# Where sublayers meet: the last half's copy behind the first low tile, and the embedding's last two copies behind the gate weights' high part

## The chip, the cores and the metric

The kernel runs on one core of one Trainium2 chip. The metric is the device time in microseconds (us); lower is better. A core has TensorE (PE, the matrix engine), VectorE (DVE), ScalarE (ACT), GpSimd (POOL) and a queue engine (SP) that issues the loads. Each takes its own instructions in the order of the program, and they meet through semaphores.

## The reference

One step of a decoder layer for 512 prompt tokens and 32 sample tokens (544 in all, in two halves of 272), model width 1024, one layer:

```python
def layer(x, p, lp, mix_fn):
    x = x + 0.5 * rmsnorm(swiglu(rmsnorm(x, lp['f1_pre']), lp['f1_in'], lp['f1_out']), lp['f1_post'])
    h = rmsnorm(x, lp['mix_pre'])
    gq, gk, gv, gg, la, sq, sk, sv = project(h, lp['w_in'], lp['gate_w'], lp['gate_b'])
    o_gla, o_sb, new_state = mix_fn(gq, gk, gv, la, sq, sk, sv)
    m = merge(o_gla, gg, o_sb, lp['gla_norm'], lp['sb_norm'], lp['w_out'], x.dtype)
    x = x + rmsnorm(m, lp['mix_post'])
    x = x + 0.5 * rmsnorm(swiglu(rmsnorm(x, lp['f2_pre']), lp['f2_in'], lp['f2_out']), lp['f2_post'])
    gate = jax.nn.sigmoid(rmsnorm(x, lp['ple_pre']) @ lp['ple_w_gate'])
    e = p.astype(x.dtype) @ lp['ple_w_up']
    x = x + rmsnorm(gate * e, lp['ple_post'])
    return x, new_state
```

Each sublayer's output is normed by its own sum of squares over the 1024 channels before it is added to x, and the new x is normed again before the next sublayer's products.

## The kernel before, in words

Channels lie on the 128 partitions, so x is 8 tiles of 128 channels by 544 tokens. Every product is done in three matmuls, of the high and low parts of both operands: activations as `a_hi` and `a_lo`, weights as a high and a low copy of what a load left in `raw`. ACT makes a high part (a rounded copy), DVE the low part (the difference). A result takes a ticket, which is one of two "quads" of four PSUM banks, in turn: ticket t has quad t % 2, and PE's `open_ticket` waits until the quad's last user has been copied out (`psum_free`).

The change lies where one sublayer ends and the next begins. There are three such edges: edge 0 (end of the first feed-forward block, then the mixer's input product), edge 1 (end of the output projection, then the second feed-forward block) and edge 2 (end of the second feed-forward block, then the gate product of the embedding). At an edge the work goes by halves of the tokens:

- PE does the last product by halves (`edge_last`). DVE copies or adds each finished half out of PSUM (`last_out(0)`, `last_out(1)`: `down_half` at edges 0 and 2, one instruction; `mix_half` at edge 1, two copies). ACT squares it (`edge_squares`), PE sums the squares over the partitions with a matmul against ones (`post_sum`), ACT turns the sum into `rstd` (`norm`).
- For each of the 8 tiles k of a half, DVE scales the output by `rstd` into `work` (L1619), adds it to x (L1625), and later makes `a_lo` of tile k - 1 (L1631). ACT makes `a_hi` (L1223) and squares x into `y` (L1225). DVE adds these squares for the next norm (L1641).
- PE's `edge_first` takes the next product's first two tickets together. For each half and each k it waits for `a_lo` of that tile and does 12 matmuls (2 tickets x 2 tiles x 3). Both quads must be free before its first matmul. It holds the second half's `post_sum` of the sublayer that ended, and behind k = 2 of its second half the first half's sum of the next norm (`pre_sum`, L573 and L574). Then `edge_second` does the third ticket.

At edge 2 four products of the embedding p @ w_up (`embed`, L695) stand on PE between `edge_last` and `edge_first`. ACT copies each of the four results out of PSUM into `e` (`e_tiles`, L1553), between its other work at the edge (`between`). The gate product's second weight block is split there too: high part on ACT (L1152), low part on DVE (L1599).

All orders are written out by hand; no scheduler moves them. The argument `between` is given at edge 2 alone, so that `if between` means edge 2 and `if not between` means edges 0 and 1.

Of the kernel before, what the change touches and what calls it, by code (L numbers as in the profile page):

```python
# [111 lines left out]
def build(nc, a, o):  # L112
# [13 lines left out]
    with ctx:  # L126
# [220 lines left out]
        def placed(name, st):  # L347

            w = W0[name] + st.c
            return PLACED.get(w, slot_pair(w)) if isinstance(st.i, int) else slot_pair(w)  # L350
# [17 lines left out]
        def ticket(st, name):  # L368


            base = T0[name]
            return base + st.n, st.parity(base), st.half(base)
# [136 lines left out]
        def _(pe):  # L509
            mm = nc.tensor.matmul  # L510

            def open_ticket(t, quad, use):

                pe.wait_ge(psum_free[quad], use)
# [4 lines left out]
            def weights(w):  # L519
                pe.wait_ge(sig["split_lo"], w + 1)  # L520
# [16 lines left out]
            def dense_half(quad, pair, tiles, k, n_k, rhs, half, width=P):  # L537

                stride, tok = tiles * width, slice(half * HALF, (half + 1) * HALF)
                for c in range(tiles):  # L540
                    cols = slice(k * stride + c * width, k * stride + (c + 1) * width)
                    for n, (wt, act) in enumerate(((pair[0], rhs[0]), (pair[0], rhs[1]), (pair[1], rhs[0]))):
                        last = mm(PS[0:width, 4 * quad + 2 * c + half, 0:HALF], wt[:, cols], act[:, k, tok],  # L543
                                  start=(k == 0 and n == 0), stop=(k == n_k - 1 and n == 2))
                return last
# [9 lines left out]
            def post_sum(j, half):  # L555


                quad, tok, summed = sum_quad[j], slice(half * HALF, (half + 1) * HALF), SUMMED[j]
                pe.wait_ge(sig["sq_used"], SQ_BASE[j] + summed)
                for k in range(summed - 1, KD):  # L560
                    if k == summed:
                        pe.wait_ge(sig["edge_sq"], 2 * (j // 2) + half + 1)
                    squares = sum_sq if k < summed else sq[:, k % 2, :]
                    last = mm(PS[:, 4 * quad + 2 + half, 0:HALF], ones[:], squares[:, tok],  # L564
                              start=(k < summed), stop=(k == KD - 1))
                last.then_inc(sig["sum_full"], 1)

            def pre_sum(j, half):


                quad, at_ = sum_quad[j], half * HALF
                pe.wait_ge(sig["pre_ready"], j - 2 + half + 1)
                mm(PS[:, 4 * quad + half, HALF:512], ones[:], sum_sq[:, at_:at_ + TAIL], start=True, stop=True)  # L573
                mm(PS[:, 4 * quad + 2 + half, HALF:2 * HALF - TAIL], ones[:], sum_sq[:, at_ + TAIL:at_ + HALF],  # L574
                   start=True, stop=True).then_inc(sig["sum_full"], 1)
# [20 lines left out]
            def edge_first(b, stage_no, sums=True):  # L596


                name = EDGES[b]
                both = [(ticket(Step(c), name), placed(name, Step(c))) for c in range(2)]  # L600
                weights(W0[name] + 1)
                for (t, quad, use), pair in both:
                    open_ticket(t, quad, use)
                for half in range(2):
                    for k in range(KD):
                        pe.wait_ge(sig["a_lo_ready"], A_BASE[stage_no] + 8 * half + k + 1)
                        for (t, quad, use), pair in both:
                            last = dense_half(quad, pair, 2, k, KD, (a_hi, a_lo), half)
                            if half and k == KD - 1:
                                last.then_inc(sig["psum_full"], 1)  # L610
                        if half and k == 2:
                            pre_sum(2 * b + 2, 0)
                        elif sums and not half and k == 0:
                            post_sum(2 * b + 1, 1)

            def edge_second(b, width=P):
# [527 lines left out]
        def _(act):  # L1144
# [17 lines left out]
            def split_edge(name, c, t):  # L1162

                st = Step(c)
                act.wait_ge(sig["psum_full"], t)
                split_into(placed(name, st), st, name, widths[W0[name] + c])
# [27 lines left out]
            def edge_squares(b, half):  # L1194


                j = 2 * b + 1
                name, c = LAST[b]
                t, quad, use = ticket(Step(c), name)
                tok = slice(half * HALF, (half + 1) * HALF)  # L1200
                if half == 0:
                    act.wait_ge(sig["sq_used"], SQ_BASE[j] + SUMMED[j])
                    act.wait_ge(sig["y_half"], b + 1)
                else:
                    act.wait_ge(psum_free[quad], use + 1)
                if SUMMED[j] == KD - 1:
                    ins = fn(sq[:, 1, tok], y[:, KD - 1, half, :], ACT.Square)
                else:
                    ins = fn(sq[:, :, tok], y[:, KD - 2:KD, half, :], ACT.Square)
                ins.then_inc(sig["edge_sq"], 1)  # L1210

            def edge(b, name, between=None):


                j, c0 = 2 * b + 1, VEC[name]
                edge_squares(b, 0)
                norm(j, 0)
                edge_squares(b, 1)
                for half in range(2):
                    for k in range(KD):  # L1220
                        act.wait_ge(sig["x_ready"], 16 * b + 8 * half + k + 1)
                        xt = x[:, k, half, :]
                        fn(a_hi[:, k, half * HALF:(half + 1) * HALF], xt, ACT.Copy,  # L1223
                           scale=vec[:, c0 + k:c0 + k + 1]).then_inc(sig["a_hi_ready"], 1)
                        fn(y[:, k, half, :], xt, ACT.Square).then_inc(sig["pre_sq"], 1)  # L1225
                        if half == 0 and k == (0 if between else 4):
                            norm(j, 1)
                        elif half == 1 and k == 4:
                            norm(j + 1, 0)
                        if between:  # L1230
                            between(half, k)
# [322 lines left out]
                   ACT.Copy).then_inc(psum_free[t % 2], 1)  # L1554

            def between(half, k):
                if half == 0 and k % 2:
                    e_tiles(k // 2)
                if half == 0 and k == 4:
                    split_edge("gate", 1, T0["f2_down1"] + KD)  # L1560
                if half and k == 2:
                    split_edge("gate", 2, T0["embed"] + 3)

# [3 lines left out]
            for n in range(3):  # L1567
# [3 lines left out]
                for c in range(2):  # L1571
                    k = 2 * n + c
# [3 lines left out]
                for c in range(2):  # L1576
                    k = 2 * n + c
# [13 lines left out]
        def _(dve):  # L1591
# [35 lines left out]
            def edge_low(b, half, k, pre, stage_no):  # L1627

                c, tok = VEC[pre] + k, slice(half * HALF, (half + 1) * HALF)
                dve.wait_ge(sig["a_hi_ready"], A_BASE[stage_no] + 8 * half + k + 1)  # L1630
                v.scalar_tensor_tensor(a_lo[:, k, tok], x[:, k, half, :], vec[:, c:c + 1], a_hi[:, k, tok].bitcast(F32),  # L1631
                                       ALU.mult, ALU.subtract).then_inc(sig["a_lo_ready"], 1)
# [12 lines left out]
            def edge(b, post, pre, stage_no, last_out, between=None):  # L1645


                last_out(0)
                for half in range(2):
                    dve.wait_ge(sig["rstd_ready"], 2 * (2 * b + 1) + half)  # L1650
                    for k in range(KD):
                        if k > 1:

                            dve.wait_ge(sig["x_ready"], 16 * b + 8 * half + k - 1)
                        edge_update(b, half, k, post)
                        if k > 2:
                            edge_add(b, half, k - 2)
                        elif half and k:

                            edge_add(b, 0, KD - 3 + k)  # L1660
                        edge_x(b, half, k)
                        if half == 0 and k == 0:
                            last_out(1)
                        if k:
                            edge_low(b, half, k - 1, pre, stage_no)
                        if between:
                            between(half, k)
                    edge_low(b, half, KD - 1, pre, stage_no)
# [498 lines left out]
            def between(half, k):  # L2167
                if half == 0 and k == 4:
                    split_edge("gate", 1)
                if half and k == 4:  # L2170
                    split_edge("gate", 2)
# [3 lines left out]
            for n in range(3):  # L2175
# [21 lines left out]
                for c in range(2):  # L2197
                    k = 2 * n + c
# [269 lines left out]
```

## Time and profile before

| what | value |
|---|---|
| median of 3 runs | 1255.69 us (1255.69 to 1261.52) |
| profiled execution, its own time | 1254.07 us |
| profiled execution, span of the core | 1252.3 us |
| PE busy | 1206.0 us, 96% of the span |
| PE weight loads busy | 1166.8 us, 93% |
| DVE busy | 601.6 us, 48% |
| ACT busy | 440.6 us, 35% |
| POOL busy | 104.5 us, 8% |
| PE idle on `e` before `edge_first` of edge 2 | 6.2 us |
| PE idle on `a_lo` at edges 0 and 1, together | 4.7 us |

The span is what the trace covers; the execution's own time is 1.8 us longer. Busy shares are means over the whole span, in which nearly all stretches are bound by PE. What the edges cost has to be read from PE's idle stretches there. The granted clock is that of TensorE, 1.00 being its full 2.4 GHz and 0.50 its lower level of 1.2 GHz.

### The profile page before, as it was taken

The page shows a single profiled execution, that of the slowest core. Times are in us where ns is not written, and L with a number is a line of the kernel's source. Part 1 is how long each engine was busy: PE and PEld are TensorE (multiplying, and loading weights), DVE is VectorE, ACT ScalarE, POOL GpSimd, SP SyncE. Part 2 cuts the span into 40 slices and gives each one's busy share as a digit, 9 for nine tenths or more (in the row PEclk, how much of TensorE's full clock was granted, in tenths as well). Part 3 has the DMA queues.
Part 4 walks back from the last instruction along what each step waited for, and adds up shares of the span by engine and source line. Part 5 has one row for each costly group of instructions (what it writes and reads, how often), then busy time and mean ns, then how long its engine had stood idle before and what let it go on. Part 6 is the DMA issues. An engine that isn't in the chain of part 4 may idle for free.

```text
span 1252.3 us, 22655 instructions
## 1 busy us (share of the span) xinstructions
PE 1206.0 (96%) x9582; PEld 1166.8 (93%) x9582; DVE 601.6 (48%) x810; ACT 440.6 (35%) x566; POOL 104.5 (8%) x147
## 2 busy tenths in 40 slices
PE   7999999999999899999998999999999999999895
PEld 6899999999999889999877698999999999999794
DVE  5443422234334857555378747544321344434737
ACT  4322222212223432312299745322221222223634
POOL 7100000000001002121040020000000000011002
PEclk9999999999999999999999999999999999999898
DMA  5223132332223122123055151223223222125102
GB/s 208 80 88 100 51 102 84 101 101 67 76 75 121 51 69 78 65 64 106 1 188 192 62 169 35 68 68 100 75 76 105 82 100 90 53 85 172 40 1 71
DMA packets 40804, 110.17 MB, mean 88 GB/s; under 512 B 4962, under 2 KB 7026, under 8 KB 40610
## 3 DMA queue, kind: packets, MB, share of 16 engines
q1 hardware_dynamic: 38930, 103.13, 25.0%
q0 software_dynamic: 1232, 5.01, 1.2%
q8 instruction: 49, 0.80, 0.3%
q10 hardware_dynamic: 576, 1.08, 0.2%
q14 instruction: 17, 0.14, 0.0%
HBM read 103.57 MB, written 5.64 MB: 87 GB/s over the span
## 4 chain that ended last, share of the span: by engine, by line
PE 88%; ACT 5%; DVE 4%; issue 1%; DMA 1%; SPq 0%; DVEq 0%; ACTq 0%
PE PS L532 70%; PE PS L543 10%; PE PS L788 1%; DVE w_lo L1599 1%; PE PS L564 1%; PE PS L815 1%; ACT w_hi L1152 1%; DMA raw<-in_w_in 1%; PE PS L695 0%; PE PS L845 0%; PE PS L889 0%; PE PS L964 0%; PE PS L848 0%; DVE extra L2230 0%; ACT proj L1359 0%
## 5 line engine op out<-in xcount | busy, mean ns | idle before, releaser
L532 PE MATMUL PS<-a_hi,w_hi 128*128 128x272 f32 x1680 | 352.1, 291 | 12.0 <-DVE w_lo L1772 7.2
L532 PE MATMUL PS<-a_lo,w_hi 128*128 128x272 f32 x1680 | 349.5, 289 | 0.0
L532 PE MATMUL PS<-a_hi,w_lo 128*128 128x272 f32 x1680 | 347.9, 288 | 0.0
L532 PEld LDWEIGHTS PS<-a_hi,w_hi 128*128 128x128 f32 x1680 | 264.6, 189 | 16.9 <-issue 11.9
L1599 DVE TENSOR_TENSOR w_lo<-raw,w_hi 128x2048 fp32r<-128x2048 f32 (+3 forms) x94 | 180.9, 1924 | 188.8 <-ACT w_hi L1152 188.8
L532 PEld LDWEIGHTS PS<-a_hi,w_lo 128*128 128x128 f32 x1680 | 265.8, 190 | 0.0
L532 PEld LDWEIGHTS PS<-a_lo,w_hi 128*128 128x128 f32 x1680 | 265.6, 190 | 0.0
L1152 ACT ACTIVATE w_hi<-raw 128x2048 fp32r<-128x2048 f32 (+3 forms) x95 | 151.5, 1595 | 75.0 <-PE PS L532 63.7
L1255 ACT ACTIVATE work<-work 128x544 f32<-128x544 f32 x44 | 29.0, 659 | 325.2 <-DVE work L1697 325.2
L1697 DVE TENSOR_TENSOR work<-PS,rstd 128x544 f32<-128x544 f32 x43 | 31.2, 726 | 210.2 <-PE PS L532 201.3
L532 PE MATMUL PS<-h_hi,w_hi 128*128 128x272 f32 x584 | 121.1, 289 | 0.0
L532 PE MATMUL PS<-h_lo,w_hi 128*128 128x272 f32 x584 | 120.8, 288 | 0.0
L532 PE MATMUL PS<-h_hi,w_lo 128*128 128x272 f32 x584 | 119.5, 286 | 0.0
L532 PEld LDWEIGHTS PS<-h_lo,w_hi 128*128 128x128 f32 x584 | 91.9, 189 | 0.0
L532 PEld LDWEIGHTS PS<-h_hi,w_lo 128*128 128x128 f32 x584 | 91.7, 188 | 0.0
L532 PEld LDWEIGHTS PS<-h_hi,w_hi 128*128 128x128 f32 x584 | 91.1, 188 | 0.0
L543 PE MATMUL PS<-a_hi,w_hi 128*128 128x272 f32 x224 | 66.8, 298 | 11.0 <-ACT e L1553 6.2
L2277 POOL COPY sum_sq<-sq 128x544 f32<-128x544 f32 x4 | 3.2, 792 | 763.1 <-ACT sq L1273 685.7
L543 PE MATMUL PS<-a_hi,w_lo 128*128 128x272 f32 x224 | 65.8, 294 | 0.0
L543 PE MATMUL PS<-a_lo,w_hi 128*128 128x272 f32 x224 | 65.5, 292 | 0.0
L543 PEld LDWEIGHTS PS<-a_hi,w_hi 128*128 128x128 f32 x224 | 43.1, 192 | 11.9 <-issue 11.8
L1705 DVE TENSOR_TENSOR h_lo<-work,h_hi 128x544 f32 (+1 forms) x43 | 31.2, 726 | 38.9 <-ACT h_hi L1257 38.9
(419 smaller groups left out, 1562.1 us busy)
## 6 DMA issues: line engine op xcount, KB each, us to landing
raw<-in_f_in SPq DMA_DIRECT2D x86, 512.0 KB, 4.5
raw<-in_f_out SPq DMA_DIRECT2D x32, 384.0 KB, 3.4
raw<-in_f_out SPq DMA_DIRECT2D x32, 320.0 KB, 3.1
raw<-in_w_rest SPq DMA_DIRECT2D x40, 256.0 KB, 2.9
raw<-in_w_out SPq DMA_DIRECT2D x8, 512.0 KB, 4.2
raw<-in_ple_w_gate SPq DMA_DIRECT2D x8, 512.0 KB, 4.1
x<-in_x SPq DMA_DIRECT2D x8, 272.0 KB, 6.9
out<-x SPq DMA_DIRECT2D x8, 272.0 KB, 2.2
```

Source lines behind the costliest of these rows:

```text
L532: last = mm(PS[0:width, 4 * quad + 2 * c + half, 0:HALF], wt[:, cols], act[:, k, half * HALF:(half + 1) * HALF], start=(k == 0 and n == 0) ...
L543: last = mm(PS[0:width, 4 * quad + 2 * c + half, 0:HALF], wt[:, cols], act[:, k, tok], start=(k == 0 and n == 0), stop=(k == n_k - 1 and n ...
L564: last = mm(PS[:, 4 * quad + 2 + half, 0:HALF], ones[:], squares[:, tok], start=(k < summed), stop=(k == KD - 1))
L788: last = mm(PS[:, 2 + hh, tok], k_[r, tok], q_[r, tok], start=True, stop=True)
L815: last = mm(PS[:, 7, n * 256:n * 256 + 256], kl_batch[:, 2 * part + n, :], gv_new[:, p * 256:(p + 1) * 256], start=True, stop=True)
L1152: fn(pair[0][:, 0:width], raw[:, slot, 0:width], ACT.Copy).then_inc(sig["split_hi"], 1)
L1255: fn(gs, gs, ACT.Silu).then_inc(sig["silu_ready"], 1)
L1599: v.tensor_tensor(pair[1][:, 0:width], raw[:, slot, 0:width], pair[0][:, 0:width].bitcast(F32), ALU.subtract).then_inc(sig["split_lo"], 1)
L1697: v.tensor_tensor(gs, banks(quad, 0, 2), r, ALU.mult).then_inc(sig["g_ready"], 1)
L1705: v.tensor_tensor(h_lo[:, hs, :].rearrange("p a t -> p (a t)"), flat(us), h_hi[:, hs, :].bitcast(F32).rearrange("p a t -> p (a t)"), ALU.s ...
L2277: g.tensor_copy(sum_sq[:], sq[:, 0, :] if j else flat(y[:, 0])).then_inc(sig["sq_used"], 1)
```

## The change

Four places are edited; nothing is added to or taken from the computation.

1. On PE, at edges 0 and 1, the second half's `post_sum` moves from behind tile k = 0 to behind tile k = 1.
2. On ACT, at edges 0 and 1, the squares of the last half (`edge_squares(b, 1)`) move from ahead of the first tile to behind tile 1. Edge 2 keeps its order.
3. On DVE, at edges 0 and 1, the last half's copy (`last_out(1)`) moves from behind x of tile 0 to behind the first low tile.
4. On ACT, at edge 2, `e_tiles(2)` and `e_tiles(3)` move from tiles k = 5 and k = 7 to directly behind the high part of the gate product's second weight block, at k = 4.

```diff
@@ PE, edge_first @@
                         if half and k == 2:
                             pre_sum(2 * b + 2, 0)
-                        elif sums and not half and k == 0:
+                        elif sums and not half and k == 1:
                             post_sum(2 * b + 1, 1)
@@ ACT, edge @@
                 norm(j, 0)
-                edge_squares(b, 1)
+                if between:
+                    edge_squares(b, 1)
                 for half in range(2):
...
                         fn(y[:, k, half, :], xt, ACT.Square).then_inc(sig["pre_sq"], 1)
+                        if not between and half == 0 and k == 1:
+                            edge_squares(b, 1)
                         if half == 0 and k == (0 if between else 4):
                             norm(j, 1)
@@ ACT, between @@
-                if half == 0 and k % 2:
+                if half == 0 and k in (1, 3):
                     e_tiles(k // 2)
                 if half == 0 and k == 4:
                     split_edge("gate", 1, T0["f2_down1"] + KD)
+                    e_tiles(2)
+                    e_tiles(3)
@@ DVE, edge @@
                         edge_x(b, half, k)
-                        if half == 0 and k == 0:
+                        if between and half == 0 and k == 0:
                             last_out(1)
                         if k:
                             edge_low(b, half, k - 1, pre, stage_no)
+                        if not between and half == 0 and k == 1:
+                            last_out(1)
```

ACT at edge 2, from `e_tiles(1)` on, before the change. `h_lo<-raw` is the high part of the gate weights (it is kept in memory of `h_lo`), `e<-PS` is an `e_tiles`:

```order
L1553 ACTIVATE e<-PS 128x1088
L1223 ACTIVATE a_hi<-x,vec 128x272
L1225 ACTIVATE y<-x 128x272
L1152 ACTIVATE h_lo<-raw 128x2048
L1223 ACTIVATE a_hi<-x,vec 128x272
L1225 ACTIVATE y<-x 128x272
L1553 ACTIVATE e<-PS 128x1088
L1223 ACTIVATE a_hi<-x,vec 128x272
L1225 ACTIVATE y<-x 128x272
L1223 ACTIVATE a_hi<-x,vec 128x272
L1225 ACTIVATE y<-x 128x272
L1553 ACTIVATE e<-PS 128x1088
```

The same place in the changed kernel:

```order
L1556 ACTIVATE e<-PS 128x1088
L1224 ACTIVATE a_hi<-x,vec 128x272
L1226 ACTIVATE y<-x 128x272
L1152 ACTIVATE h_lo<-raw 128x2048
L1556 ACTIVATE e<-PS 128x1088 x2
L1224 ACTIVATE a_hi<-x,vec 128x272
L1226 ACTIVATE y<-x 128x272
L1224 ACTIVATE a_hi<-x,vec 128x272
L1226 ACTIVATE y<-x 128x272
L1224 ACTIVATE a_hi<-x,vec 128x272
L1226 ACTIVATE y<-x 128x272
```

The two last copies now stand ahead of the high parts of tiles 5, 6 and 7; they stood behind those of tiles 5 and 7.

DVE at edge 1, from x of tile 0 on, before the change. `y<-PS` is the copy of the last half, and the line with `a_lo` is the first low tile:

```order
L1625 TENSOR_TENSOR x<-work,x 128x272
L1746 COPY y<-PS 128x272 x2
L1619 SCALAR_TENSOR_TENSOR work<-y,vec,rstd 128x272
L1625 TENSOR_TENSOR x<-work,x 128x272
L1631 SCALAR_TENSOR_TENSOR a_lo<-x,vec,a_hi 128x272
```

The same place in the changed kernel:

```order
L1630 TENSOR_TENSOR x<-work,x 128x272
L1624 SCALAR_TENSOR_TENSOR work<-y,vec,rstd 128x272
L1630 TENSOR_TENSOR x<-work,x 128x272
L1636 SCALAR_TENSOR_TENSOR a_lo<-x,vec,a_hi 128x272
L1753 COPY y<-PS 128x272 x2
```

The scaling, the sum and the low part now stand ahead of the copies. Edge 0 has the same order with one `y<-PS,y` (L1734) in place of the two copies. On ACT the squares `sq<-y` move at both edges from ahead of `a_hi` of tile 0 to behind the square of tile 1.

## Rows read from the trace of the kernel before

**Rows 1.** The page, part 4: shares of the chain that ended last, by engine
```profile
PE 88%; ACT 5%; DVE 4%; issue 1%; DMA 1%; SPq 0%; DVEq 0%; ACTq 0%
```

**Rows 2.** PE's waits: line, releaser, us in total, times, longest
```profile
PE PS L543 <- ACT e L1553: 6.2, 1, 6.2
PE PS L543 <- DVE a_lo L1631: 4.7, 2, 2.6
...
PE PS L564 <- ACT sq L1207: 1.4, 1, 1.4
```

**Rows 3.** Chain at edge 1: start us, us, what
```profile
759.25 0.80 DVE y L1746 x2
...
760.08 0.66 ACT sq L1209
...
761.83 1.75 PE PS L543 x12
763.58 1.38 PE PS L564 x6
764.95 15.10 PE PS L543 x120
```

**Rows 4.** DVE in order of time, edge 1: start, us, line, operation
```profile
757.03 0.44 DVE L1625 TENSOR_TENSOR x<-work,x 128x272 f32<-128x272 f32 x1
...
760.49 0.44 DVE L1625 TENSOR_TENSOR x<-work,x 128x272 f32<-128x272 f32 x1
...
762.49 0.50 DVE L1631 SCALAR_TENSOR_TENSOR a_lo<-x,vec,a_hi 128x272 fp32r<-128x272 f32 x1
```

**Rows 5.** ACT in order of time, edge 1: the norm of the second half
```profile
766.42 0.47 ACT L1178 ACTIVATE rstd<-PS,eps 128x272 f32<-128x272 f32 x1
```

**Rows 6.** DVE in order of time, edge 0
```profile
416.59 0.44 DVE L1734 TENSOR_TENSOR y<-PS,y 128x272 f32<-128x272 f32 x1
416.94 0.50 DVE L1619 SCALAR_TENSOR_TENSOR work<-y,vec,rstd 128x272 f32<-128x272 f32 x1
417.47 0.44 DVE L1625 TENSOR_TENSOR x<-work,x 128x272 f32<-128x272 f32 x1
417.94 0.50 DVE L1631 SCALAR_TENSOR_TENSOR a_lo<-x,vec,a_hi 128x272 fp32r<-128x272 f32 x1
```

**Rows 7.** PE in order of time, edge 0: first matmul, its idle time ahead
```profile
418.59 0.41 PE L543 MATMUL PS<-a_hi,w_hi 128*128 128x272 f32 x1 [2.04 <-DVE a_lo L1631]
```

**Rows 8.** Chain at edge 2
```profile
1181.97 18.98 PE PS L543 x132
1200.95 0.41 PE PS L573 x2
```

**Rows 9.** ACT in order of time, edge 2
```profile
1171.47 1.91 ACT L1152 ACTIVATE h_lo<-raw 128x2048 fp32r<-128x2048 f32 x1
...
1180.66 1.06 ACT L1553 ACTIVATE e<-PS 128x1088 f32<-128x1088 f32 x1
```

**Rows 10.** DVE in order of time, edge 2: weights' low part, low tiles, x
```profile
1173.41 2.29 DVE L1599 TENSOR_TENSOR h_lo<-raw,h_lo 128x2048 fp32r<-128x2048 f32 x1 [3.04 <-ACT h_lo L1152]
...
1176.38 0.44 DVE L1625 TENSOR_TENSOR x<-work,x 128x272 f32<-128x272 f32 x1
1176.73 0.50 DVE L1631 SCALAR_TENSOR_TENSOR a_lo<-x,vec,a_hi 128x272 fp32r<-128x272 f32 x1
...
1191.36 0.50 DVE L1631 SCALAR_TENSOR_TENSOR a_lo<-x,vec,a_hi 128x272 fp32r<-128x272 f32 x1
```

**Rows 11.** Windows: stretch, length, busy PE, PEld, DVE, ACT, POOL, PEclk, DMA
```profile
418.59:421.49 2.90, 2.90 (x13) 2.90 (x14) 2.87 (x8) 1.81 (x6) 0.00 (x0) 0.53 0.00 0
759.22:763.58 4.36, 1.75 (x13) 1.78 (x14) 4.01 (x10) 2.97 (x7) 0.00 (x0) 1.00 0.00 0
1175.75:1181.97 6.22, 0.00 (x2) 0.03 (x1) 6.01 (x16) 4.42 (x9) 0.00 (x0) 0.84 0.50 169
1181.97:1186.80 4.83, 4.83 (x21) 4.83 (x22) 4.83 (x14) 3.87 (x7) 0.00 (x0) 0.50 0.02 3
```

## The prediction

> **What bounds the kernel now.** I read the page first. The chain that ended last lies on PE for 88% of the span [rows 1], so nearly every stretch is paid in matmuls, and a reordering can give back only time in which PE stands still or runs at its lower clock. The second view is what PE waits for [rows 2]. Two of its entries lie at the edges that the change touches: 6.2 us at edge 2, where the first gate product waits for a copy of the embedding (`e`), and 4.7 us at edges 0 and 1 together, where `edge_first` waits for its first low tile. The larger of those two is 2.6 us, so the other is 2.1. The third view is the timeline of each engine around the three edges, and the fourth is the granted clock there [rows 11]. What is to be seen in them stands with each edge below.
>
> **Edge 2: the two embedding copies (ACT).** PE's last embedding matmul ends at 1175.75 and the first gate matmul starts at 1181.97: the idle window has that length, 6.22 us, with no PE work in it [rows 11]. What ends it is the last of the four copies: it starts at 1180.66 and takes 1.06, so it ends at 1181.72 [rows 9], and PE follows 0.25 later [rows 8]. That copy is late only because ACT reaches it behind tile 7, and tile 7 waits for DVE. DVE in turn had been held until 1175.70 by the low part of the gate weights (1173.41 + 2.29) [rows 10]. In the changed order both copies stand behind the weights' high part, which ends at 1171.47 + 1.91 = 1173.38 [rows 9]. The first copy can run there at once, to about 1174.4. The second needs the last embedding product, which ends at 1175.75. It starts at about 1175.78, ends 1.06 later at 1176.84, and PE follows by the same 0.25, at 1177.09. The weights' low part is then ready by 1.4 us. The start comes 1181.97 - 1177.09 = 4.88 us earlier, and the idle time falls from 6.22 to 1.34.
>
> Does PE find its tiles? The low tiles of k = 0 to 3 were done before DVE took the weights' low part, and that of k = 4 ends at 1176.73 + 0.50 = 1177.23 [rows 10]. From there on DVE makes a low tile in about 1.5 us (16 instructions in 6.01 us, four to a tile [rows 11]), and PE uses one in 15.10 / 120 x 12 = 1.51 us [rows 3]. PE starts four tiles behind DVE, so it doesn't catch up. DVE's later halt for the second weight block is the place to look at: the low tile k = 4 of the second half ends at 1191.36 + 0.50 = 1191.86 [rows 10]. PE at full clock needs it after 12 tiles and the first `pre_sum`, at about 1177.09 + 0.24 + 12 x 1.51 + 0.55 = 1196.0. There are 4 us to spare. What ACT has waiting behind the two copies is the high part of tile 5, which needs x of tile 5; that is done at 1176.38 + 0.44 = 1176.82 [rows 10], and ACT is free at 1176.84. So holding ACT for the last embedding product costs nothing. The last three tiles of the second half wait for the norm behind `pre_sum`, so they move along with it.
>
> The clock is the second part of this edge. Behind the idle 6.22 us PE ran its first 4.83 us at a granted clock of 0.50, and did 21 matmuls in them, 0.23 each against 0.126 at 1.00 [rows 3, 11]. Its 132 matmuls up to `pre_sum` took 18.98 [rows 8]. At edge 1 the same kind of matmuls, 12 and then 120, took 1.75 + 15.10 = 16.85 at full clock, and there the engine had stood still 2.61 us just before them, without losing its clock [rows 3, 11]. An idle 1.34 us, in the midst of dense matmuls on both sides, is half of that, so I take full clock: 18.98 - 16.85 = 2.13 us more. Edge 2 gives 4.88 + 2.13 = 7.01 us. The bounds of the clock term are 0 (it still falls, and PE pays as much as before) and 2.13.
>
> The Trainium skill, page "TensorE: Matmul & The Clock Gate", section "A second HAM failure mode: psum-queue depth-cycling", speaks against taking that whole term: a PE that idles briefly between groups of matmuls can fall back to the lower clock again and again. By that rule the sum would lack 2.13 us; by the row of edge 1, which kept 1.00 through a longer pause, it has it. The row decides for me, and the rule is a rival below.
>
> **Edge 1: squares, copy and sum.** Before, x of tile 0 was done at 757.03 + 0.44 = 757.47 [rows 4], but ACT had the last half's squares ahead of `a_hi`, and these had to wait for DVE's copies, which start at 759.25 right behind PE's last matmul (at 761.83 - 2.61 = 759.22) and end at 759.25 + 0.80 = 760.05. The squares ended at 760.08 + 0.66 = 760.74 [rows 2, 3], `a_hi` and `a_lo` of tile 0 followed, and PE started at 761.83 [rows 3]. In the new order `a_lo` of tile 0 is ready by about 758.8, before PE ends the last product. This doesn't let PE start at 759.23, though. `edge_first` opens both quads before its first matmul, and one of them is the quad of the last output product, which DVE's copies free at 760.05. DVE reaches them in time: x, scaling, x and low part are done some 1.8 us after 757.03. With 0.14 us for the signal (the low tile of edge 0 ends at 418.44, PE starts at 418.59 [rows 6, 7]) PE starts at 760.2. The gain is 761.83 - 760.2 = 1.63 us, out of the 2.61 of idle time. The bounds are 1.5 (a signal as slow as the 0.25 of edge 2 [rows 8, 9]) and 1.65.
>
> Behind that, the second low tile must follow. After the copies DVE does scaling and x of tile 2 (before, the x in this position started at 760.49 [rows 4]), then the low part at 760.49 + 0.35 = 760.84, done at 761.34. PE wants it after 12 matmuls in 1.75, at 761.95, so it is 0.6 us early. It started at 762.49 before [rows 4]: all of DVE's work from there on is 1.65 us earlier, as is PE's. The moved `post_sum` costs its 1.38 us behind tile 1 in place of tile 0 [rows 3]; no matmul is added. It ends at 760.2 + 1.75 + 1.51 + 1.38 = 764.84. ACT asks for it before its norm at 766.42 [rows 5] less 1.65, which is 764.77: 0.1 us of waiting, in front of a norm that DVE needs only 3 us later. Edge 1 gives 1.6 us.
>
> **Edge 0.** Here DVE isn't held by PE: PE's last product of this edge ends at about 416.55, and the copy ran at 416.59 [rows 6], right behind x of tile 0. In the new order scaling starts at 416.59, x 0.53 later (as 416.94 to 417.47), the low part 0.35 behind that (as 416.59 to 416.94), at 417.47, and the copy behind it, between 0.35 and 0.50 later by the spacings and lengths of these rows; I take 0.41, so 417.88. It ends at 418.32 and frees the quad. PE starts 0.14 later, at 418.46, where it started at 418.59 [rows 7]. So the copy takes the place of the low tile as what PE waits for, and the gain is 0.13 us. The clock there is 0.53 in the first 2.90 us [rows 11]; `post_sum` moves from the end of that stretch to behind it and tile 1 moves in, which exchanges matmuls of one engine in a stretch that isn't made longer. I take nothing for it. The bounds are 0 and 1.4 us, the latter if the clock doesn't fall: 13 matmuls in 2.90 against 1.75 for 12 at edge 1, and the slow rest of the sum. ACT waits for the later `post_sum` there, by about 1 us, ahead of the norm; DVE is still at tile 5 then and uses that norm about 3 us later.
>
> **The sum.** 7.01 + 1.6 + 0.13 = 8.75 us. Everything behind each edge is PE's own work, or the same chain behind `pre_sum`, and moves along. No load moves past another one: the gate weights' loads are released by the low parts, which stay where they are. The profiled execution took 1254.07, so 1254.07 - 8.75 = 1245.3 for an execution like it. The median of the runs shown is 1.6 us above it, so 1246.9 for a median. I take 1246.9.
>
> **The rivals.**
> (a) *The short pause at edge 2 still costs the clock* (10%). For it: edge 0, where a pause of 1.4 us for the squares came shortly ahead of the one of 2.04, got 0.53 [rows 2, 7, 11]. Against it: edge 1. Then edge 2 gives 4.88 alone, the sum is 6.6 and the time 1249.1.
> (b) *The edges 0 and 1 give nothing, or edge 2 is held elsewhere* (13%). The first part alone costs 1.7: 1248.6. For the second, the place is PE's start behind the weights' low part or a tile: if the tiles of the second half are late, each microsecond of it is given back one to one, up to the whole 7. The time would be about 1252. Against it: the 4 us of slack at tile 4 of the second half.
> (c) *Slower* (2%). The one mechanism that I can name is ACT held by the wait of the second copy at edge 2, with `a_hi` of tiles 5 to 7 queued behind it. The price is one to one for what the last embedding product ends later than x of tile 5, less PE's lead of four tiles. By the rows the product ends 1.07 us before x of tile 5 (1175.75 against 1176.82) and the copy fits in exactly. The wait decides from about 6 us on, when tile 5 would be late on PE. To lose 0.5% it would have to be some 20 us.
> (d) *The forecast, with the clock at full level* (75%).
>
> **How the numbers follow.** A measurement of this kernel can tell about 0.5% (6.3 us, so 1249.4) from no change. Case (d) lies clearly below it, (a) and the milder half of (b) just below, where the scatter of a median may put them on either side. Faster 0.86, same 0.12, slower 0.02. The range takes (d) with the clock kept at edge 0 (1246.9 less 1.4, and less the 1.6 that a median may not have over the profiled execution: 1243.9) and, on the other side, (a) with edge 1 at nothing (1250.8). That is 1243.8 to 1250.8.
>
> **What would show it.** In the trace of the changed kernel PE's wait for `e` at edge 2 should be 1.3 us in place of 6.2, the granted clock 1.00 behind it, and 132 matmuls should take about 16.9. At edge 1 PE's pause should be about 1.0 us, ended by the copy `y` and no longer by `a_lo`. At edge 0 it should still be 1.9, ended by `y` as well, with a low clock behind it. The prediction is wrong if the clock at edge 2 is 0.50 again, if a wait for `a_lo` appears in `edge_first`, or if PE stands still behind `post_sum`.

## The result, and the profile after

The changed kernel took 1247.64 us (median of 5, 1247.5 to 1248.74); the kernel before took 1259.18 (median of 5, 1255.69 to 1261.52). The ratio is 0.9935, with a 95% interval of 0.9919 to 0.995. A repetition of both on one chip gave 0.9936 (0.9922 to 0.995). That is 8.2 us less of 1256. The two medians of five are 11.5 us apart, but the five executions of the kernel before are spread over 5.8 us, and larger sets of it (17, 7 and 11 executions) have medians of 1255.43, 1255.56 and 1256.2; so I go by the ratio. The prediction had 8.75 less, and 1246.9 us.

The profiled execution of the changed kernel has a span of 1245.2 us, 7.1 us less than before. Its waits of PE, as in [rows 2] (line, releaser, us in total, times, longest):

```profile
PE PS L543 <- DVE y L1741: 2.0, 1, 2.0
...
PE PS L543 <- ACT e L1556: 1.4, 1, 1.4
PE PS L564 <- ACT sq L1207: 1.2, 1, 1.2
PE PS L543 <- DVE y L1753: 1.1, 1, 1.1
```

The wait for `e` at edge 2 fell from 6.2 to 1.4 us. At edges 0 and 1 PE waits no longer for `a_lo` but for DVE's copy `y`: 1.1 us at edge 1 (2.6 before), and 2.0 at edge 0, as before [rows 7]. The chain at edge 2, which answers to [rows 8]:

```profile
1164.14 10.56 PE PS L695 x84
...
1174.72 1.09 ACT e L1556
...
1176.05 16.84 PE PS L543 x132
1192.89 0.41 PE PS L573 x2
```

The last copy starts when the last embedding product ends and PE follows it. The windows of the pause and of the 132 matmuls, in the columns of [rows 11]:

```profile
1174.70:1176.05 1.35, 0.00 (x0) 0.03 (x1) 1.35 (x4) 1.33 (x2) 0.00 (x0) 1.00 0.25 39
1176.05:1192.89 16.84, 16.84 (x133) 16.84 (x134) 15.59 (x36) 8.07 (x17) 0.00 (x0) 1.00 0.18 60
```

The granted clock is 1.00 in both, where it was 0.50 behind the pause before [rows 11]. The chain at edge 1, which answers to [rows 3]:

```profile
755.83 3.76 PE PS L543 x30
...
759.62 0.80 DVE y L1753 x2
...
760.66 3.27 PE PS L543 x24
763.93 1.37 PE PS L564 x6
765.30 9.82 PE PS L543 x78
```

ACT's squares and the low tile are gone from the chain; only DVE's copy stands between PE's last product and its next one.

To compare executions, I cut each trace at the same points of the program. "Edge 0" and "edge 1" run from the first half's sum of squares (L564) to the first matmul of tile 2; "edge 2" from the first embedding matmul to `pre_sum` (L573); "head" is what lies ahead of edge 0, "tail" what lies behind edge 2's `pre_sum`. Each is the difference of two starts in the chain. For edge 2 before: 1200.95 - 1162.79 = 38.16. In the order of before, tile 2 has no row of its own: the chain's row starts with tile 1, and I add the 1.51 us of its 12 matmuls. For edge 0 before: 422.81 + 1.51 - 413.95 = 10.37. All in us; "slow" marks a spell of TensorE's clock at 0.50 within an edge.

| profile | head | edge 0 | edge 1 | edge 2 | tail | span |
|---|---|---|---|---|---|---|
| before | 413.95 | 10.37 slow | 12.36 | 38.16 slow | 51.4 | 1252.3 |
| before, second | 415.28 | 10.20 slow | 12.37 | 38.47 slow | 51.3 | 1254.0 |
| changed | 415.91 | 8.81 | 10.84 | 31.17 | 52.3 | 1245.2 |
| changed, second | 414.63 | 8.82 | 10.84 | 31.17 | 52.3 | 1243.8 |
| changed, third | 413.89 | 10.33 slow | 10.83 | 31.18 | 52.2 | 1244.5 |

Edge 1 gives 1.53 us, to a few hundredths the same each time. Edge 2 of the changed kernel repeats to 0.01 us, that of the kernel before differs by 0.3 (its slow 132 matmuls took 18.98 and 19.29), so edge 2 gives 7.0 to 7.3. Edge 0 moves by 1.5 us among executions of the changed kernel, and the head by 1.3 and 2.0 among executions of one and the same kernel. The tail is the same within each kernel and 0.9 us longer in the changed one.

### The profile page after: what moved, and what is told of

The parts are those of the page before. It is cut to its first block, busy times and chain, and to the rows that moved or that the text cites. A ratio compares the mean times of both kernels' runs of the same rounds, so it can differ in the third digit from the quotient of the medians.

```text
span 1245.2 us, 22655 instructions
## 1 busy us (share of the span) xinstructions
PE 1204.4 (97%) x9582; PEld 1164.5 (94%) x9582; DVE 601.9 (48%) x810; ACT 441.2 (35%) x566; POOL 104.5 (8%) x147
## 4 chain that ended last, share of the span: by engine, by line
PE 89%; DVE 5%; ACT 4%; DMA 1%; issue 1%; ACTq 0%; SPq 0%; DVEq 0%
PE PS L532 70%; PE PS L543 10%; PE PS L788 1%; PE PS L695 1%; PE PS L964 1%; DVE w_lo L1604 1%; PE PS L564 1%; PE PS L815 1%; ACT w_hi L1152 1%; DMA raw<-in_w_in 1%; DMA raw<-in_f_in 1%; PE PS L845 0%; PE PS L889 0%; PE PS L848 0%; DVE extra L2237 0%
## 5 line engine op out<-in xcount | busy, mean ns | idle before, releaser
L532 PEld LDWEIGHTS PS<-a_hi,w_hi 128*128 128x128 f32 x1680 | 264.9, 189 | 18.5 <-issue 12.5
L1267 ACT ACTIVATE y<-PS 128x544 f32 (+1 forms) x16 | 10.0, 627 | 106.5 <-PE PS L532 106.5
```

## The experiments

**Edge 2 alone.** The kernel before, with part 4 of the change:

```diff
-                if half == 0 and k % 2:
+                if half == 0 and k in (1, 3):
                     e_tiles(k // 2)
                 if half == 0 and k == 4:
                     split_edge("gate", 1, T0["f2_down1"] + KD)
+                    e_tiles(2)
+                    e_tiles(3)
```

> The kernel before with the embedding's two last copies moved (part 4 of the change) and nothing else. Theory: nearly all of the gain lies here. PE's wait for e at edge 2 falls from 6.2 to about 1.4 us, the granted clock behind it is 1.00, 132 matmuls take about 16.85 us in place of 18.98, and the time is 7.0 us below before (a ratio of about 0.9945). PE's pause at edge 1 stays 2.6 us. Rival, that the move gives only its place and the clock term was a matter of the single execution: 4.9 us (0.996). Rival, that the three parts at edges 0 and 1 carry the gain: within 0.2 per cent of before.

The ratio is 0.9942 (0.9929 to 0.9955), 7.3 us. Edge 1 took 12.36 as before, edge 2 took 31.18 as in the changed kernel. Its chain:

```profile
1177.08 16.84 PE PS L543 x132
1193.92 0.41 PE PS L573 x2
```

This start is the forecast's 1177.09, in an execution whose embedding products begin at 1162.74 as before. Both rivals of this run fall: the gain is at edge 2, and the clock term is in it. Edge 0 took 10.37, with the slow spell.

**Edges 0 and 1 alone.** The changed kernel with that diff reversed.

> The changed kernel with the embedding's copies put back to tiles 5 and 7 (parts 1 to 3 of the change alone). Theory: 1.5 us at edge 1 and nothing at edge 0, so 1.5 us below before (a ratio of about 0.999), not to be told from before by the time alone. PE waits at edge 1 for the copy y, 1.1 us, and at edge 2 for e, 6.2 us, with the clock at 0.50 behind it. Rival, edges carry the gain: 4 us or more below before.

The ratio is 0.9983 (0.9974 to 0.9992), 2.1 us. Its waits:

```profile
PE PS L543 <- ACT e L1556: 6.2, 1, 6.2
...
PE PS L543 <- DVE y L1751: 1.1, 1, 1.1
```

Edge 1 took 10.83, as in the changed kernel, and edge 2 37.57, slow. Edge 0 took 8.81, without the spell, in this profile. The 2.1 us have an interval of 1.0 to 3.3, in which the expected 1.5 lies. The two parts' gains, 7.3 and 2.1, add up to 9.4, which agrees with the whole 8.2 within the intervals.

**The squares without DVE's copy.** The changed kernel, with `last_out(1)` back behind x of tile 0:

```diff
-                        if between and half == 0 and k == 0:
+                        if half == 0 and k == 0:
                             last_out(1)
                         if k:
                             edge_low(b, half, k - 1, pre, stage_no)
-                        if not between and half == 0 and k == 1:
-                            last_out(1)
```

> The changed kernel with DVE's copy of the last half put back ahead of the first low tile at edges 0 and 1; the squares on ACT and the sum on PE stay moved. Theory: DVE's copy then holds scaling, x and low part behind it, so that PE starts at edge 1 with the low tile, about 1.3 us behind the copy's end in place of 0.25: the pause there is 2.2 to 2.3 us, against 1.1 in the changed kernel and 2.6 before. Edge 0: first matmul 4.6 us behind the first half's sum of squares, as before and as in the changed kernel. Rival, that the moved squares alone free PE: pause 1.1 us.

```profile
759.14 0.79 DVE y L1751 x2
759.93 0.42 DVE work L1624
...
760.37 0.44 DVE x L1630
760.81 0.42 DVE a_lo L1636
...
761.37 3.25 PE PS L543 x24
```

This is the chain at edge 1. With only the squares moved, scaling, x and low part run behind the copy, and PE's pause is 2.3 us, as expected; edge 1 takes 12.02. So of the 1.53 us the squares, with PE's moved sum, carry 0.34 and the order on DVE 1.2. At edge 0 the first matmul came 4.52 us behind the sum of squares (418.57 - 414.05), 0.1 less than expected and 0.12 less than in the kernel before and in the changed one (4.64 in both): there the moved squares gain 0.12 us, and DVE's copy, put behind the low tile, takes it back. Edge 0 as a whole took 10.21, with the slow spell. DVE's order can't be tried without the squares moved: the copy would wait for a low tile whose high part waits for squares of that copy.

**The last copy one and two tiles later.** The changed kernel with `e_tiles(3)` behind tile 5, and behind tile 6:

```diff
                     e_tiles(2)
+                if half == 0 and k == 5:
                     e_tiles(3)
```

> The changed kernel with the last of the embedding's four copies one tile later, behind tile k = 5 in place of k = 4. Theory: the copy ends when tile 5 is through on ACT, about 1.9 us later than in the changed kernel, so PE's pause at edge 2 is 3.1 to 3.3 us. Whether TensorE keeps its clock then is open: edge 1 kept 1.00 through 2.61 us, edge 0 got 0.5 in one execution behind two pauses of 3.5 us in all. Clock kept: pre_sum comes 1.9 us later than in the changed kernel. Clock lost: about 3.5 us later.

> The changed kernel with the last embedding copy behind tile k = 6. Theory: PE's pause at edge 2 is 4.7 us (copy ends one tile, 1.5 us, later than behind tile 5) and the clock falls, so pre_sum comes 3.4 us and the cost of a slow clock, 2 to 2.7 us, later than in the changed kernel: 36.7 to 37.2 us from the first embedding matmul. Clock kept: 34.6.

Windows of the pause and behind it, with the copy behind tile 5:

```profile
1175.70:1178.89 3.19, 0.03 (x2) 0.04 (x1) 3.19 (x9) 2.06 (x4) 0.00 (x0) 0.88 0.55 141
1178.89:1185.00 6.11, 6.11 (x27) 6.11 (x28) 5.90 (x16) 3.48 (x10) 0.00 (x0) 0.51 0.25 101
```

The trace names `a_lo` as what ended this pause, but the copy `e` is what PE waits for: the low tile named is that of tile 5, and PE's first matmul needs tile 0. The copy ends at 1177.58 + 1.06 = 1178.64 and PE follows 0.25 later, as behind the other copies `e`; the low tile happens to end 0.1 us behind it. Which wait ended has to be asked of the program there. The pause was 3.2 us and the clock fell within it; edge 2 took 35.66, 4.5 more than in the changed kernel, where 3.5 was expected with the clock lost: 1.8 of later start and 2.7 of slow matmuls (19.53 for the 132). Behind tile 6 the pause was 4.7 and edge 2 took 37.26, 6.1 more, a little above what was expected (19.61 for the 132). With the copies at tiles 4, 5, 6 and 7 the pause is 1.35, 3.2, 4.7 and 6.2, and edge 2 takes 31.17, 35.66, 37.26 and 38.2. The step from the first to the second is the largest, since it loses the clock as well. Beyond that the clock's cost doesn't grow with the pause (2.7 and 2.8 us at the two middle ones, 1.6 to 2.5 in the profiles with 6.2).

**The gap filled.** Two kernels on the order before, both with the third copy moved up and the fourth left at tile 7; the second also has matmuls in the gap:

```diff
                 weights(W0[name] + 1)
+                if b == 2:
+                    open_ticket(*both[0][0])
+                    for n in range(50):
+                        mm(PS[:, 4 * both[0][0][1], 0:240], w_hi[:, W0["gate"] % 2, 0:P], a_hi[:, 0, 0:240],
+                           start=True, stop=True)
                 for (t, quad, use), pair in both:
```

> The kernel before with the third embedding copy moved to directly behind the weights' high part and the fourth left at tile 7. It is the control for the filled gap. Theory: PE still waits for the fourth copy, 6.2 us, the clock falls, and 132 matmuls take about 19 us.

> As the control, with 50 matmuls of 240 columns added on PE in the gap ahead of the first gate matmul; they write into PSUM columns that the gate product overwrites, so the result is the same. Theory of the clock: the added matmuls take about 5.5 us, end before the fourth copy does and move nothing, but the clock stays 1.00, so the 132 matmuls take 16.85 us and the kernel is about 2.1 us faster than the control in spite of doing more work. Rival, that the slow matmuls come from the operands (low tiles or weights just written) and not from the idle time: 19 us as in the control.

The control's windows (pause, 132 matmuls), then those of the filled gap:

```profile
1177.30:1183.54 6.24, 0.02 (x2) 0.03 (x1) 6.03 (x16) 3.57 (x8) 0.00 (x0) 0.84 0.51 168
1183.54:1202.53 18.99, 18.99 (x133) 18.99 (x134) 10.93 (x24) 5.71 (x11) 0.00 (x0) 0.87 0.00 1
```

```profile
1177.08:1183.14 6.06, 5.87 (x51) 5.70 (x51) 5.85 (x16) 3.50 (x7) 0.00 (x0) 1.00 0.54 176
1183.14:1199.98 16.84, 16.84 (x133) 16.84 (x134) 11.09 (x25) 5.81 (x11) 0.00 (x0) 1.00 0.00 1
```

With the gap filled by useless work, the same 132 matmuls take 16.84 in place of 18.99, and edge 2 takes 35.87 in place of 38.18 (the other 0.16 us is an earlier start). The slow matmuls come from the idle time, not from their operands. This measures the clock term by itself: 2.15 us. The times of the two single runs, 1253.84 and 1255.75, lie 1.9 apart.

**Edge 0 filled.** The kernel before, with 15 such matmuls in PE's pause at edge 0 (`if b == 0`, moving operand `h_hi`):

> The kernel before with 15 matmuls of 240 columns added on PE in its pause at edge 0, into PSUM columns that the product overwrites. In all four profiles so far of the kernels with the order before at all three edges' first tiles (before twice, the control and the filled gap of edge 2) and in that of the edge-2 part alone, the clock fell at edge 0, and the stretch from the first half's sum of squares to tile 2 took 10.2 to 10.4 us; in the changed kernel's three profiles it took 8.8 twice and 10.3 once. Theory, idle time takes the clock: with the pause filled no spell at edge 0, 8.8 to 8.9 us. Rival, the order of sum and tiles decides it: 10.2 to 10.4 us, as in the unfilled kernel.

```profile
419.37 1.74 PE PS L543 x12
421.11 0.92 PE PS L564 x4
422.03 4.03 PE PS L543 x32
```

This is its chain behind the filled pause: twelve matmuls in 1.74 us, where they took 2.9 at a clock of 0.53 before [rows 11]. Edge 0 took 8.81 us. The order of the sum and the tiles is the one of before, so that order does not by itself bring the slow spell. That the spell needs the idle time is what this one profile speaks for, beside five of five with the spell where the pause wasn't filled; one profile can't show that a filled pause never has one.

**The changed kernel twice more, and the one before.** No edit.

> The changed kernel itself once more, next to the kernel before on the same chip, for its time and a second profile. Theory: edges 1 and 2 take the same to 0.1 us as in its first profile (10.8 us from the first sum of squares to tile 2 at edge 1, 31.2 us from the first embedding matmul to pre_sum at edge 2), while the slow spells of TensorE's clock at 41 us, at edge 0 and in the tail may lie otherwise, each worth 0.9 to 1.9 us. Ratio to before 0.993 to 0.995. Rival, the clock's spells belong to the order of the program: this profile shows the same spells as the first (one at 41 us, none at edge 0).

> The changed kernel once more for a third profile. Same theories as for the second: edges 1 and 2 fixed, spells at 41 us, at edge 0 and in the tail free; or all spells as in the first profile.

> The kernel before once more for a second profile. Theory: edge 1 takes 12.4 us and edge 2 38.2 us as before, with 1.8 to 2.7 us of it the slow clock; the spell at edge 0 may be there or not.

The stretches are in the table above; edges 1 and 2 came as expected, but for edge 2 of the kernel before, which took 0.3 us more. The third profile of the changed kernel has the spell at edge 0 that its first two have not:

```profile
418.53 4.77 PE PS L543 x24
```

The same 24 matmuls take 3.26 at full clock. The spell at 41 us is in the first two and not in the third, and of the kernel before it is in the second profile and not in the first. So these spells do not belong to the order of the program alone.

**Quad by quad.** A further version: `edge_first` opens its second quad only when the first has work behind it.

```diff
-                weights(W0[name] + 1)
-                for (t, quad, use), pair in both:
-                    open_ticket(t, quad, use)
+                lead = 1 if sums else 2
+                weights(W0[name])
+                (t, quad, use), pair = both[0]
+                open_ticket(t, quad, use)
+                for k in range(lead):
+                    pe.wait_ge(sig["a_lo_ready"], A_BASE[stage_no] + k + 1)
+                    dense_half(quad, pair, 2, k, KD, (a_hi, a_lo), 0)
+                (t, quad, use), pair = both[1]
+                weights(W0[name] + 1)
+                open_ticket(t, quad, use)
+                for k in range(lead):
+                    dense_half(quad, pair, 2, k, KD, (a_hi, a_lo), 0)
+                if sums:
+                    post_sum(2 * b + 1, 1)
                 for half in range(2):
-                    for k in range(KD):
+                    for k in range(0 if half else lead, KD):
...
-                        elif sums and not half and k == 1:
-                            post_sum(2 * b + 1, 1)
```

> The changed kernel with edge_first opening its two quads one after the other: at edges 0 and 1 ticket 0 does its 6 matmuls of tile 0 before ticket 1's quad is waited for, and the second half's sum of squares goes back behind tile 0; at edge 2 ticket 0 does tiles 0 and 1 (12 matmuls) first. Theory, that the pauses of the changed kernel at edge 1 and edge 2 are waits for the second quad alone: at edge 1 the first matmul follows the last product at once, gain 1.0 us; at edge 2 the wait for e vanishes under 1.5 us of matmuls, gain 1.3; at edge 0 0.3 to 0.6 us. In all 2.5 to 2.9 us below the changed kernel, 1245 us. Rival, that PE waits for the low tiles or the weights and not for the quads: the pauses stay, same time as the changed kernel.

The ratio to the kernel before is 0.9901 (0.9884 to 0.9918), and the median 1242.55 us; the changed kernel's is 0.9935. Edge 2's chain has no pause any more:

```profile
1160.03 10.54 PE PS L704 x84
1170.57 16.61 PE PS L543 x132
1187.18 0.41 PE PS L573 x2
```

Edge 2 took 29.57 (1.60 less than in the changed kernel; 1.3 expected), edge 1 9.97 (0.87 less; 1.0), edge 0 8.34 (0.47 less; 0.3 to 0.6): 2.9 us in all. The pauses that the change left at edges 1 and 2 were waits for the second quad, as the prediction had it for edge 1: at edge 1 0.21 us of the 1.07 is left, at edge 2 nothing. At edge 0 PE still waits 1.6 us, for the first low tile. The gain at edge 2 is 0.25 us more than the pause of 1.35, and the timeline of PE shows why. The first gate matmuls in the changed kernel, behind the pause:

```profile
1176.05 0.36 PE L543 MATMUL PS<-a_hi,w_hi 128*128 128x272 f32 x1 [1.37 <-ACT e L1556]
1176.25 0.29 PE L543 MATMUL PS<-a_lo,w_hi 128*128 128x272 f32 x1
```

The same in the quad-by-quad version, without one:

```profile
1170.41 0.29 PE L543 MATMUL PS<-a_hi,w_hi 128*128 128x272 f32 x1
1170.54 0.30 PE L543 MATMUL PS<-a_lo,w_hi 128*128 128x272 f32 x1
```

By these rows each matmul of a stream lasts 0.29 us, but the next one starts after 0.13, so they overlap: the first gate matmul starts at 1170.41, before the last embedding one ends at 1170.57. Behind a pause this overlap of 0.16 is lost, and the second matmul starts 0.20 behind the first and not 0.13. So a pause costs 0.23 us more than its idle time. The two ratios lie 4.3 us apart, but their intervals are wide enough for 2.9.

## Why the prediction was right or wrong

- **Edge 2, the copies.** Right. From the first embedding matmul to the first gate matmul it was 1181.97 - 1162.79 = 19.18 before and 1176.05 - 1161.72 = 14.33 after: 4.85 us, against 4.88. No tile, weight block or held ACT was late.
- **Edge 2, the clock.** Right. The 132 matmuls took 16.84, against 16.85; the filled gap shows that idle time is the cause. Rival (a) fell: a pause of 1.35 us kept 1.00 in five profiles (the changed kernel three times, the edge-2 part alone, the squares alone). At 3.2 us, in the kernel with the last copy behind tile 5, it was lost. The Trainium skill, "TensorE: Matmul & The Clock Gate", section "A second HAM failure mode: psum-queue depth-cycling", tells of a kernel in which PE idles briefly between groups of matmuls so often that its clock swings between the two levels. The trace doesn't agree with carrying that over to one pause of 1.35 us, behind which the clock was 1.00; pauses that recur as often as that are in no run here.
- **Edge 1.** The mechanism was right, the size 0.1 too large: 1.53 for 1.63. I had taken 0.14 us from the copy's end to PE, and it was 0.24, the bound that the prediction named.
- **Edge 0.** The copy does take the low tile's place, but the start did not move at all: it came 4.64 us behind the sum of squares in both kernels (418.59 - 413.95 and 420.55 - 415.91), since the signal again took 0.1 us more than I had taken. The prediction's sign for this edge, a pause of 1.9 us "with a low clock behind it", failed in its second half: the pause was 2.03 us, and behind it the clock was kept in two of three profiles. The chain of the changed kernel:

```profile
419.94 0.36 DVE y L1741
...
420.55 3.26 PE PS L543 x24
```

- **The step that failed** is edge 0's clock, "I take nothing for it", and with it the clause of the sum that everything behind each edge moves along. At edge 0 the sum had 0.13 us from an earlier start and 0 from the clock; measured were 0.00 from the start, and 1.4 to 1.6 from the clock in the two profiles that kept it. The prediction had named this as a bound (1.4) and left it out. What lies outside the edges was taken as unchanged and wasn't. In the first pair of profiles the three edges gave 6.99 + 1.52 + 1.56 = 10.1 us, the head lost 1.96 (it moves by 2.0 within the changed kernel too) and the tail 0.9, and what is left of it in the spans is 7.1 and not 8.75. Of the head's 1.96 us, 0.7 is lost before 41 us at a clock of 1.00 in both, and the rest behind it, where the granted clock from 41.0 to 44.5 us was 1.00 before and 0.52 in the changed kernel.

The tail lost 0.9, at the last sum of squares, in all three profiles of the changed kernel. In the one before:

```profile
1240.45 1.32 PE PS L564 x4
```

In the changed one, where the clock falls just ahead of it (1.00 up to 1232.35, then 0.50):

```profile
1232.39 2.20 PE PS L564 x4
```

This slow last sum (2.0 to 2.2 us) came also with edges 0 and 1 alone, with the squares alone and with the filled gap. It didn't come in the other six experiments' profiles (1.2 to 1.3), three of which have the changed edges 0 and 1 or more. So it is no fixed price of the change; what decides it stays open.

The two kernels' means over the five profiles of the table differ by 8.65 (1253.15 less 1244.5). The measured 8.2 agrees with that.
- **Edge 0's spell in the two orders stays open.** In the order before it came in five profiles of five without a fill there (before twice, the edge-2 part, the control and the filled gap of edge 2). In the changed order, with edge 2 as it may be, it came in two of six (the third of the changed kernel, and the one with the last copy behind tile 5). With the squares alone moved it came too, in the one profile. The pause itself is the same 2.0 us. Whether the order has a share in this or it is chance, these runs don't settle.
- **The median.** 1247.64 against 1246.9, within the range. That this is so near is in part luck. For the profiled execution the prediction had 1245.3, and it took 1247.64, 6.4 us less than before and not 8.75. The 1.6 us put on for the median was a guess from three runs of before and measured 0: in this kernel the profiled execution's time and the median are the same 1247.64. The two errors nearly cancelled.
- **How clear the gain is.** The prediction put case (d) "clearly below" the 0.5% that a measurement can tell. The ratio's interval reaches from 0.9919 to 0.995, and its upper end is just that line. "Clearly" was too strong.
- **The other rivals.** (b) fell with edge 1's 1.53 us and edge 2's 4.85 of earlier start; (c) fell, since ACT held by the second copy made nothing late.

## What to carry to other kernels

When an engine pauses at a junction, look for the instruction that ends the pause and ask what stands ahead of it in its engine's queue without being needed by it: two copies of 1.06 us, moved from behind slower work to where their data was ready, were worth 7 us, of which 2.1 was the clock that the long pause had cost. Then look at the next wait in line before expecting all of the pause back: at edge 1 the low tile was ready 0.5 us early, but PE waited for both PSUM quads, though its first matmuls write only to the one that was free, and that kept 1.1 of the 2.6 us. And cut the traces of several executions at fixed points before judging a term of one or two microseconds: where no slow spell came, the edges repeated to 0.1 us, while the spans of one kernel moved by 1.4.

## What the runs showed of the hardware

- How long a pause takes the clock, for one pause between dense matmuls: it was kept at 1.35 us (five profiles) and at 2.6 (the six profiles with the order of before at edge 1), and lost at 3.2, 4.7 and 6.2. Two pauses of 0.7 to 1.4 and 2.04 us shortly behind one another (edge 0) lost it in some executions and kept it in others.
- A fall costs what PE has to do in the slow spell: 1.6 to 2.8 us at edge 2, 1.4 to 1.6 at edge 0, 0.9 in the tail. Two profiles (the last copy behind tile 6, and edge 0 filled) had a spell at 530 us, amid small matmuls of the mixer, of 2.5 and 1.5 us, where the others had none. The Trainium skill, "TensorE: Matmul & The Clock Gate", section "Part 1: The HAM clock gate", says of the start of a kernel that its count of slow matmuls varies from run to run. Here the same holds in the middle of one: the changed kernel had a spell at edge 0 in one profile and none in two.
- From DVE's copy to PE's first matmul it was 0.24 us where PE had another wait, already fulfilled, behind the one for the quad, and 0.14 in the quad-by-quad version, where the matmul follows that wait directly. It was 0.14 too where the low tile, PE's last wait, ended the pause (edge 1 before: 761.18 + 0.51 to 761.83). That the second wait costs the 0.1 us is a reading of these cases, not tested alone:

```profile
756.48 0.80 DVE y L1762 x2
757.27 0.14 issue
757.41 0.98 PE PS L543 x6
```

- A pause costs more than its idle time: 0.23 us more, by the rows of the quad-by-quad version. Twelve matmuls behind a pause took 1.74 to 1.75 us at a clock of 1.00, and 1.51 within a stream.
